# Two residual blocks on one core: the boundaries with a norm between two stages, reordered by token block

## The reference, cut to what matters

```python
# first block: for each of two layers
h = h + mixer(rms_norm(h, attn_norm))            # hgrn2_mixer, then dsa_mixer (sparse attention)
h = h + conv_ffn(rms_norm(h, ffn_norm))          # SwiGLU with a causal convolution of width 3
h = rms_norm(h, final_norm)
# second block: for each of two layers
f = swiglu(rms_norm_2(h, ffn_pre_g), ...);  h = h + 0.5 * rms_norm_2(f, ffn_post_g)
m = mixer(rms_norm_2(h, mix_pre_g));        h = h + rms_norm_2(m, mix_post_g)   # gmlp_mixer, then mla_mixer
f = swiglu(rms_norm_2(h, ffn_pre_g), ...);  h = h + 0.5 * rms_norm_2(f, ffn_post_g)
# shared_kv(h) is computed between the two layers of the second block
```

## Time and profile before

| | us |
|---|---|
| median of 3 runs (lowest, highest) | 1752.01 (1750.46, 1755.83) |
| the profiled execution's own time | 1747.85 |
| its span, first to last instruction | 1746.0 |

### The profile page before, as it was taken

One profiled execution on the slowest core, in us unless ns is written; L12 is line 12 of the kernel. 1 busy time (PEld: TensorE's weight loads), 2 busy tenths in 40 slices (PEclk: granted clock), 3 DMA queues, 4 the chain that ended last, 5 costly groups with the idle time before them and its releaser, 6 DMA issues.

```text
span 1746.0 us, 32509 instructions
## 1 busy us (share of the span) xinstructions
PE 1667.6 (96%) x12061; PEld 1535.6 (88%) x12061; DVE 1140.6 (65%) x1899; ACT 890.2 (51%) x1411; POOL 25.6 (1%) x72
## 2 busy tenths in 40 slices
PE   7999999998999998999899989998899998989998
PEld 6888999896799997999889789998899988689997
DVE  4768777775587777555647765556655557565555
ACT  6455655564565556444556454444644444464443
POOL 4000000000000000000000000000000000000000
PEclk9999999997999999999999999999999999799999
DMA  8446666672366667666465546665466664136662
GB/s 245 140 134 195 200 183 180 182 150 73 97 182 187 184 181 229 180 186 187 144 217 170 182 153 190 185 180 168 133 192 181 181 187 138 53 117 194 185 186 72
DMA packets 393755, 292.73 MB, mean 168 GB/s; under 512 B 33403, under 2 KB 365588, under 8 KB 393296
## 3 DMA queue, kind: packets, MB, share of 16 engines
q1 hardware_dynamic: 390160, 279.79, 55.0%
q0 software_dynamic: 2816, 10.24, 1.7%
q10 hardware_dynamic: 704, 1.67, 0.3%
HBM read 290.59 MB, written 1.07 MB: 167 GB/s over the span
## 4 chain that ended last, share of the span: by engine, by line
PE 91%; DVE 5%; ACT 2%; issue 1%; DMA 1%; SPq 0%; DVEq 0%; ACTq 0%
PE ps L389 28%; PE ps L390 28%; PE ps L391 28%; PE ps L446 1%; DVE w_lo L380 1%; DVE H L549 1%; PE ps L1925 1%; PE ps L1924 1%; DMA raw<-in_hgrn_w_in 1%; PE ps L855 0%; ACT L526 0%; PE ps L1389 0%; DVE SQ L542 0%; PE ps L1654 0%; DVE A L1569 0%
## 5 line engine op out<-in xcount | busy, mean ns | idle before, releaser
L389 PE MATMUL ps<-x_hi,w_hi 128*128 128x256 f32 x2672 | 762.4, 285 | 6.5 <-DVE x_lo L473 2.5
L390 PE MATMUL ps<-x_hi,w_lo 128*128 128x256 f32 x2672 | 758.8, 284 | 0.0
L391 PE MATMUL ps<-x_lo,w_hi 128*128 128x256 f32 x2672 | 758.5, 284 | 0.0
L380 DVE TENSOR_TENSOR w_lo<-raw,w_hi 128x1024 fp32r<-128x1024 f32 x532 | 646.2, 1218 | 33.9 <-ACT w_hi L373 33.3
L373 ACT ACTIVATE w_hi<-raw 128x1024 fp32r<-128x1024 f32 x532 | 542.4, 1047 | 81.6 <-PE ps L391 72.5
L389 PEld LDWEIGHTS ps<-x_hi,w_hi 128*128 128x128 f32 x2672 | 515.5, 193 | 14.0 <-issue 6.4
L390 PEld LDWEIGHTS ps<-x_hi,w_lo 128*128 128x128 f32 x2672 | 515.5, 193 | 4.5
L391 PEld LDWEIGHTS ps<-x_lo,w_hi 128*128 128x128 f32 x2672 | 515.1, 193 | 0.0
L659 ACT ACTIVATE sl<-gs 128x256 f32<-128x256 f32 x88 | 37.0, 421 | 397.7 <-DVE gs L763 397.7
L763 DVE TENSOR_TENSOR gs<-ps,R 128x256 f32<-128x256 f32 x88 | 37.3, 424 | 277.0 <-PE ps L391 277.0
L389 PE MATMUL ps<-w_hi,h_hi 128*128 128x512 f32 x528 | 207.1, 392 | 1.3 <-DVE h_lo L687 1.3
(11 more groups left out here) (279 smaller groups left out, 1315.5 us busy)
## 6 DMA issues: line engine op xcount, KB each, us to landing
raw<-in_ffn_w_up SPq DMA_DIRECT2D x176, 512.0 KB, 3.8
raw<-in_ffn_w_down SPq DMA_DIRECT2D x132, 512.0 KB, 4.5
raw<-in_ffn_w_gate SPq DMA_DIRECT2D x88, 512.0 KB, 4.6
raw<-in_hgrn_w_in SPq DMA_DIRECT2D x32, 512.0 KB, 4.8
raw<-in_gmlp_w_in SPq DMA_DIRECT2D x32, 512.0 KB, 4.5
raw<-in_gmlp_w_out SPq DMA_DIRECT2D x16, 512.0 KB, 4.0
raw<-in_hgrn_w_out SPq DMA_DIRECT2D x8, 512.0 KB, 3.6
raw<-in_dsa_w_in SPq DMA_DIRECT2D x16, 256.0 KB, 4.6
```

Source lines behind the costliest of these rows:

```text
L380: nc.vector.tensor_tensor(w_lo[:, s, :], raw[:, s, :], w_hi[:, s, :].bitcast(F32), ALU.subtract)\
L389: pe.matmul(o, whi, xhi, start=first, stop=False, skip_group_check=not group)
L390: pe.matmul(o, wlo, xhi, start=False, stop=False, skip_group_check=not group)
L391: return pe.matmul(o, whi, xlo, start=False, stop=last, skip_group_check=not group)
```

## The change

Six edits, all at the boundaries. `NORMED` is the list of the turns for ffn2, gmlp, ffn3, kv, mla and ffn5.

1. The last two output chunks of ffn2 to ffn5, gmlp and mla are issued by token block: block 0 of both chunks, then block 1 of both (before: all four parts of the one, then of the other).
2. `root_table`: one tiny Sqrt on ACT (128x1) ahead of the wait at the end of every FFN, and at the end of gmlp and mla, so that the function set is loaded there.
3. `pe_turn` of a `NORMED` turn transposes block 0 as soon as two quarters of `H` are there, then block 1, into banks 2 to 5 instead of 4 to 7. gmlp's value chunks move from banks 0 to 3 and 4 to 7 to 0, 1, 6, 7 and 2, 3, 4, 5, with a wait for two of the gelus ahead of its tiles 2 and 3; kv's third tile moves to bank 6 and its spread factor to bank 7.
4. `early_square`: the squares of `H`'s block 0 for the next norm move ahead of `act_turned`; `act_roots` keeps block 1.
5. `act_post` writes its (unused) squares into `gs` and `sl` instead of `SQ`; `dve_post` waits for the gain row first.
6. In ffn0 and ffn1 the `split_lo` of the last tile moves from the middle of its work to behind the last `h_lo`, where now three stand in a row.

```diff
+        warm = sb("warm", [P, 1])
+        NORMED = ["ffn2", "gm", "ffn3", "kv", "ml", "ffn5"]
+        V_BANKS = ((0, 1, 6, 7), (2, 3, 4, 5))
...
+            early = n in NORMED
+            if early:
+                pe.wait_ge(*rows_of(n, 2))
+                for k in range(KT):
+                    turn_block(pe, n, k, 0)
             for q in range(4):
                 if n != "hg":
                     pe.wait_ge(*rows_of(n, 4 if q > 1 else 2 if n in ("ffn0", "ds") else 3))
                 for k in (2 * q, 2 * q + 1):
-                    for tb in range(TB):
-                        mm = pe.transpose(ps[:, TURN_BANK[q], (k % 2) * L + tb * P:(k % 2) * L + tb * P + P],
-                                          H[:, tb, k * P:k * P + P], c_ident)
+                    for tb in range(1 if early else 0, TB):
+                        mm = turn_block(pe, n, k, tb)
                 mm.then_inc(S("turned"), 1)
+        def turn_bank(n, q):
+            return ps[:, 2 + q if n in NORMED else TURN_BANK[q], :]
...
+        def row_square(act, tb):
+            nc.scalar.activation(sq_flat[:, tb * D:tb * D + D], H[:, tb, :], ACT.Square, accum_out=ss[:, tb:tb + 1])\
+                .then_inc(S("row_sq"), 1)
+        def early_square(act, n):
+            act.wait_ge(*rows_of(n, 2))
+            row_square(act, 0)
+        def root_table(act):
+            nc.scalar.activation(warm[:, :], eps6[:, :], ACT.Sqrt)
         def act_roots(act, n):
-            for tb in range(TB):
+            for tb in range(1 if n in NORMED else 0, TB):
...
-        R_BANK = {n: {"gm": 0, "kv": 3}.get(n, 7) for n in TURNS}
+        R_BANK = {n: {"gm": 0}.get(n, 7) for n in TURNS}
+        KV_BANK = (0, 1, 6)
...
             down_part(19, 0, 19, c0 + 63)
-            down_part(20, 0, 20, c0 + 64)
-            down_part(21, 0, 21, c0 + 65)
+            if conv:
+                down_part(20, 0, 20, c0 + 64)
+                down_part(21, 0, 21, c0 + 65)
+            else:
+                for tb in range(TB):
+                    down_part(20, 0, 20, c0 + 64, (2 * tb, 2 * tb + 1))
+                    down_part(21, 0, 21, c0 + 65, (2 * tb, 2 * tb + 1))
...
             it(21, 0, 21)
+            root_table(act)
             act.wait_ge(used, c0 + 64)
             high(21, 1)
...
-                if i0 > 1:
+                if 1 < i0 < NF - 1:
                     split_lo(dve, c + 2 + AHEAD, n)
...
-            for c in (64, 65):
+            for c in (63, 64, 65) if f < 2 else (64, 65):
                 split_lo(dve, start[FN[f]] + c + AHEAD)
...
@@ att_pe of mla; gmlp_pe has the same with G2 and k @@
+                    if t < KT - 2:
+                        out_part(t).then_inc(used, 1)
+                    else:
+                        out_part(t, (0, 1))
...
+            out_part(KT - 2, (2, 3)).then_inc(used, 1)
+            out_part(KT - 1, (2, 3)).then_inc(used, 1)
...
@@ gmlp_pe @@
+                if t in (2, 3):
+                    pe.wait_ge(S("gm_v"), t + 3)
...
@@ gmlp_act; mla_act has the same @@
+            root_table(act)
             act_post(act, "gp", "gmlp")
+            early_square(act, "ffn3")
```

More of the change, by code:

```diff
@@ L408, in tok_rows @@
                 for hf in range(2):
-                    o = ps[:, banks + 2 * tb + hf, :]
+                    o = ps[:, banks[2 * tb + hf], :]
                     f = slice(hf * 512, hf * 512 + 512)
@@ L472, in dve_turned @@
                 for k in (2 * q, 2 * q + 1):
[L473 removed]
+                    nc.vector.scalar_tensor_tensor(x_lo[:, k, :], turn_bank(n, q)[:, (k % 2) * L:(k % 2) * L + L], vcol(*gain(k)),
                                                    x_hi[:, k, :].bitcast(F32), ALU.mult, ALU.subtract).then_inc(S("x_lo_done"), 1)
@@ L534, in dve_post @@
                 for hf in range(2):
+                    if not hf and not tb:
+                        dve.wait_ge(S("in_gain"), GAINS_IN[n])
                     dve.wait_ge(S("f_sq"), 4 * p + 2 * tb + hf + 1)
+                    f = slice(hf * 512, hf * 512 + 512)
                     if not hf:
@@ L603, in up_part, with down_part @@
                     mm.then_inc(used, 1)
-            def down_part(i, n, i0, c):
-                pe.wait_ge(lo_done, c + 1 + RING * n)
-                pe.wait_ge(*tile("hid_lo", f, i + 1))
+            def down_part(i, n, i0, c, part=(0, 1, 2, 3)):
+                if 0 in part:
+                    pe.wait_ge(lo_done, c + 1 + RING * n)
+                    pe.wait_ge(*tile("hid_lo", f, i + 1))
                 par = i0 % 2
-                mm = out_rows(pe, c, h_hi[:, par, :], h_lo[:, par, :], i0 == 0, i0 == NF - 1, n_)
-                mm.then_inc(used, 1)
+                mm = out_rows(pe, c, h_hi[:, par, :], h_lo[:, par, :], i0 == 0, i0 == NF - 1, n_, part)
+                if 3 in part:
+                    mm.then_inc(used, 1)
             if f != 4:
@@ L1211, in att_pe, with out_part @@
         def att_pe(pe, n, NH, per, c_out, logits, value):
+            def out_part(t, part=(0, 1, 2, 3)):
+                return out_rows(pe, c_out + t, x_hi[:, t, :], x_lo[:, t, :], t == 0, t == KT - 1, "mla", part)
             for h in range(-1, NH + 5):
@@ L1230, in att_pe @@
                     pe.wait_ge(S("at_xlo"), DSA_COUNT["xlo"] + t + 1)
-                    out_rows(pe, c_out + t, x_hi[:, t, :], x_lo[:, t, :], t == 0, t == KT - 1, {"da": "dsa", "ma": "mla"}[n])\
-                        .then_inc(used, 1)
+                    if t < KT - 2:
+                        out_part(t).then_inc(used, 1)
+                    else:
+                        out_part(t, (0, 1))
                 g = h - 3
@@ L1646, in gmlp_pe, with out_part @@
             LAG = 2
+            def out_part(k, part=(0, 1, 2, 3)):
+                return out_rows(pe, c0 + 32 + k, x_hi[:, k % KT, :], x_lo[:, k % KT, :], k == 0, k == G2 - 1, "gmlp", part)
             for g in range(G2 + LAG):
@@ L1660, in gmlp_pe @@
                     pe.wait_ge(S("gm_glo"), k + 1)
-                    out_rows(pe, c0 + 32 + k, x_hi[:, k % KT, :], x_lo[:, k % KT, :], k == 0, k == G2 - 1, "gmlp").then_inc(used, 1)
+                    if k < G2 - 2:
+                        out_part(k).then_inc(used, 1)
+                    else:
+                        out_part(k, (0, 1))
+            out_part(G2 - 2, (2, 3)).then_inc(used, 1)
+            out_part(G2 - 1, (2, 3)).then_inc(used, 1)
         def gmlp_act(act):
@@ L1939, in mla_act @@
             att_act(act, "ma", NH_M, 1, c0 + 10)
+            root_table(act)
             act_post(act, "mp", "mla")
+            early_square(act, "ffn5")
         def mla_dve(dve):
@@ L2066, in _ @@
             mid_act(act)
+            early_square(act, "ffn2")
             act_turned(act, "ffn2", lambda j: ("ffn_pre_g_2", j), start["ffn2"])
```

34 lines of the change are left out of this document (18 added, 16 removed).

## The result

| | before | changed | ratio, 95% interval |
|---|---|---|---|
| first comparison: median (runs) | 1751.24 (4) | 1730.82 (4; 1728.86 to 1735.54) | 0.9894 [0.9876, 0.9911] |
| second, with the experiments | 1751.06 (9) | 1732.92 (5; 1731.33 to 1737.90) | 0.9896 [0.9882, 0.9909] |
| profiled execution, its span | 1747.85, 1746.0 | 1731.79, 1730.0 | |

The kernel is 1% faster: 20.4 and 18.1 us by the medians, 16.1 from one profiled execution to the other. The forecast was 1735.7, 16.3 less; as a ratio 0.9907, inside both intervals.

The account below looks back on a forecast made before the run. The prediction took TensorE as the bound (91% of the chain of waits), with only waits between stages to gain. Its boundary terms sum to 16.3 us; 1752.0-16.3 = 1735.7, range 1729 to 1745.

Parts of the forecast that it names:

- mla to ffn5: Boundary after mla: load and root until 1539.6, first transpose at 1545.45, ninth step 1550.85 against 1553.48; gain 2.6 us.
- ffn1 to ffn2: Convolution end: late residual against the load leaving the chain and early transposes; +0.2 us, bounds -1 to +1.5.
- ffn0 to dsa: Convolution end: `h_hi` 0.5 late, a third `w_lo` 1.13 more, so the residual 1.6 us late; -1.6, bounds -1.6 to 0.
- T: Start of PE's first transpose (changed kernel: block 1's); 1.85 us earlier after ffn2 to ffn4, 2.3 after gmlp and ffn5.
- The early turn: Block 0's 8 transposes (1.7 us) fit before T, leaving two ahead of the first `x_hi`: 0.43 us less.
- the ninth step: Next stage's ninth step of three 256-column matmuls, marking the boundary's end; it can start at T+5.4 us, paced by `x_lo`.
- The forecast's assumption: At the turns, PE's shorter standstills (about 0.8, 0.5 and 0.4 us) let its clock stay at 2.4 GHz.
- the clock still falls: Rival at the turns: gap closes but steps run at 1.2 GHz; gain 7.7 us, time 1744.3, chance 0.15.
- E: End of PE's last output matmul in a stage; before the change T came 4.79 us later.
- the half turn: At ffn1 to ffn2, turning block 0 early was to roughly repay the delay of block 1, leaving +0.2 us.
- gmlp's 0.75: gmlp to ffn3: the last chunk's block 0 comes at 1013.15, its `x_lo` ends at 1013.87; PE stalls 0.75 us.
- the delay of 0.15: mla's end: the last `x_lo` (about 1537.6) delays PE by 0.15 us, hidden behind ACT's load and root chain.

Follow-up runs that it names:

- x10: The changed kernel run again, unedited, beside others on the same chip; 1732.92 us (5 runs).
- experiment 11: x3 plus 18 to 20 unread identity transposes on PE in the pause ahead of each late turn; 1733.62 us, ratio 0.9903.
- x1: The changed kernel without its three early table loads (`root_table` calls); 1741.15 us, ratio 0.9955.
- x2: The changed kernel with the last two output chunks in the old order, each whole, one after the other; 1742.06 us, ratio 0.9965.
- x3: The changed kernel with block 0 transposed together with block 1 instead of early; 1740.36 us, ratio 0.9954.
- x4: The changed kernel with early load and moved `split_lo` both taken back at the ends of ffn0 and ffn1; 1730.89 us, ratio 0.9904.
- x6: The changed kernel with only the early load taken back at the ends of ffn0 and ffn1; 1729.73 us, ratio 0.9875.
- x8: The changed kernel with convolution's `split_lo` back, its load behind ACT's last splits, ffn0 to ffn4's last `split_lo` later, mla's load earlier; 1726.04 us, ratio 0.9853.
- x12: x8 run again, unedited, beside the changed kernel on the same chip; 1726.55 us, ratio 0.9863.
- x7: The changed kernel with unread identity transposes filling PE's pauses at the six turns; 1732.66 us, ratio 0.9881.
- x9: x8 plus unread identity transposes in PE's pauses: 18 before ffn2's turn, 2 ffn5's, 3 others, 6 between blocks (none at ffn2); 1723.84 us, ratio 0.9842.
- x5: The changed kernel with only the moved `split_lo` taken back at the ends of ffn0 and ffn1; 1730.85 us, ratio 0.9882.

## Why the prediction was right, step by step

| term (old minus new) | predicted | measured | changed again (x10), turn alone |
|---|---|---|---|
| ffn2 to gmlp | 2.85 | 3.18 | 3.18 |
| gmlp to ffn3 | 2.5 | 2.73 (3.54 less 0.81) | 3.55 |
| ffn3 to kv | 3.8 | 4.24 | 4.25 |
| ffn4 to mla | 3.6 | 4.06 | 4.06 |
| mla to ffn5 | 2.6 | 1.11 (1.40 less 0.29) | 3.37 |
| output | 2.3 | 2.24 | 2.31 |
| ffn1 to ffn2 | +0.2 | -0.08 (0.35 less 0.43) | 1.21 |
| ffn0 to dsa | -1.6 | -1.53 (-1.17 less 0.36) | -1.17 |

The sum, 15.95 without the part outside the turns and their stages, lies so close to 16.3 partly by luck. The turns for gmlp, ffn3, kv and mla gave 1.5 more than forecast, and ffn5's 1.5 less, where the clock fell; neither was foreseen. The mechanisms, one by one:

**Order by block and the load.** T came 2.05 us earlier, not 1.85: DVE's `w_lo` did hold the chain (857.77+2.35 = 860.12, then `f_b` and two products, as said), but `H` followed the inverse 0.2 sooner than I had put it. `H` to T, 3.58, is as predicted.

**The early turn.** The first matmul came 2.04 after T (predicted 2.15) and the ninth step 5.15 (5.4), because I priced transposes at the 0.21 of a row that ran at the lower clock level. At the full level eight cost 1.09. The same row's 2.08 from T to the first `x_lo`, also in the sum, was taken at that level too. As predicted, `x_lo` paces the steps now.

**The clock.** The forecast's assumption held at four turns of five in the profiled execution and at five of five in the next; the rival "the clock still falls" would have given 1744.3 and didn't come. What I had not seen is how much of my own sum it carried. From T to L the old turns took 3.16 (gmlp), 6.34, 7.34, 7.15 and 6.95 us; the same late turns at full clock take 2.26 and four times 5.37 (experiment 11). That is 7.2 us of clock. The shorter way from E to T gives 10.1 (five times 4.79 against 2.74, 2.44, 2.74, 2.73, 3.22 in x10), the early turn 1.1. Together 18.4, as the five turns of x10 have it.

The Trainium skill ("TensorE: Matmul & The Clock Gate", "Part 4: PE-mode transpose"), by which the full clock does not engage for transposes, is not what these runs show: the windows of experiment 11 and of the changed kernel have 1.00 where PE did nothing else. At gmlp before, the granted clock of 868.50 to 869.00 is 0.78; had it come back only with the first other matmul at 868.89, it would be 0.61. The prediction calls the case where that rule holds its second rival; it is the first of its list.

The Trainium skill ("ScalarE: Activation LUTs", "What ACT_TABLE_LOAD costs") adds 1380 ns of drain to a load. The trace again has none: x1's root starts 0.01 us after its load's end (1214.44+1.28, 1215.73), and the load 0.02 us after the end of the instruction ahead of it (1214.22+0.20).

**mla to ffn5.** The forecast of T, 3.7 after E, was 0.5 too late (3.22). The loss against the forecast is the clock alone: 1.97 from T to L (7.12 against 5.15).

**The convolution's ends.** For ffn0 the sum was right and its two halves nearly (the load holds E by 0.37 where I had 0.5, the third `w_lo` costs 1.12 where I had 1.13): `h_hi` held by the load, three `w_lo` in a row, residual late. For ffn1 I expected the half turn to repay it; measured, -0.08 with the clock down for 6.8 us of that turn in both, and 0.8 (1.21 less 0.43) in x10, where it was down half as long.

**Stalls costed at a little.** gmlp's 0.75 measured 0.81, with a stall of 0.70 on `x_lo` in the trace. At mla the delay of 0.15, which was to be hidden, measured about 0.3, and x2, with the old order, has 91.59 where three profiles with the new one and the same 23.9 us at the lower level have 91.89 to 91.93. Edits 4 and 5 have no run of their own; that they are worth nothing was argued and is not shown.

**What the median adds.** Both timed differences (20.4, 18.1) lie above my 16.3. ffn5's clock is worth 2 in executions where it stays up, but x10's, which is one, was the slowest of its five runs (1737.90). The rest goes along with the mean clock, .9735 over 30 runs of before and .981 over 9 of the changed kernel, but where in those runs it was won isn't shown; no profile belongs to them.

## What the runs showed of the hardware

**At the same turn of the same kernel the clock falls in one execution and not in the next**, and the more often the longer PE stood still. Over the profiles of all kernels, of the turns for gmlp, ffn3, kv, mla and ffn5, the clock fell

| pause ahead of the first transpose | turns where the clock fell |
|---|---|
| 4.79 (before) | 5 of 5 |
| 1.3 or 1.7, then 1.0 (x1, x2); 2.4 to 3.3 in one piece (x3) | 9 of 15 (x2's at gmlp 0.4 us behind L) |
| 0.3 to 1.1, then 1.0 between the blocks (changed, x4 to x6, x10) | 3 of 25 |
| 0.3 to 0.5, then 1.0 (x8, x12) | 1 of 10 |
| filled with transposes (x7, x9, x11) | 0 of 15 |

**Outside the turns the clock falls too, and the lengths of stages go with it.** mla's stage was 90.9 to 91.2 us long in the six profiles with 20.5 us of it at the lower level, 91.6 to 91.9 in the four with 23.9, 94.3 in the three with 27.3, and 97.3 in the one with 34.1. A fall at one turn isn't simply added either: where it came at kv's turn (x1, x5, x12), none came on the way from there to ffn4's end, and that was 1.2 to 1.4 us shorter than in the profiles with one.

**The median goes loosely with the mean clock**: .9735 before (1750 us), .976 to .977 for x1, x2 and x3 (1740 to 1742), .981 for the changed kernel, .982 to .983 for x8, x9 and x12 (1724 to 1727). x7 and x11 stand out: .983 to .984 and no faster than the changed kernel, so a higher mean clock need not bring time. x4 is no slower than the changed kernel at .980, and the slowest of x10's five runs had .982. That the clock makes the medians' differences is not shown.

**A 128x128 transpose of fp32 costs 0.13 us at 2.4 GHz and 0.23 at 1.2**: sixteen in 1.97 (x11) and in 3.68 (before).

## What to carry to other kernels

When PE stands still at a boundary for some microseconds, price the work behind the pause twice, from rows at either clock level: here 7 of 18 us gained at five turns came from transposes and first steps that ran at the full level again, and the early turn, 1 us of work, cost 7 to 10 when it was undone (x3). An early table load or an early split is free only where the engine's next instruction really waits for something else; in the convolution it held `h_hi`. Moving it behind the last splits, together with the other moves of experiment 8, gave the version that beats both kernels (x8 and x12: ratio 0.985 and 0.986); the moves were not timed one by one. And take a second profile before explaining one turn by its clock.
